# A two-layer trunk on one core: the second expert stage's rows fetched by index from memory, retention's queries and keys in seven half products, and the first attention weights loaded in halves

## The chip, the cores and the metric

The kernel runs on one core of one Trainium2 chip. The metric is the device time of one execution in microseconds (us). The engines are TensorE (PE in the profile, with its weight loads PEld), VectorE (DVE), ScalarE (ACT), GpSimd (POOL) and the SyncE queue (SP), which only issues transfers here. All data is float32.

## What is computed

```python
def trunk(x, cond, ...):                       # 128 context tokens and 256 sample tokens, D = 1024
    for i in range(2):
        sh1, sc1, g1, sh2, sc2, g2 = ada_modulation(cond, w_ada[i], b_ada[i])
        h = rmsnorm(x, norm_mix_g[i]) * (1 + sc1) + sh1
        mix = diff_attention(h, ...) if i == 0 else retention(h, ...)
        x = x + g1 * mix
        h = rmsnorm(x, norm_ffn_g[i]) * (1 + sc2) + sh2
        x = x + g2 * group_moe(h, w_router, router_bias, moe_w_gate[i], moe_w_up[i], moe_w_down[i])
    return rmsnorm(x, final_norm_g), ...

def retention(h, w_qkv, w_g_f, w_g_b, ...):    # 4 heads, query and key width 256, value width 512
    q, k, v = split(h @ w_qkv); g_f = silu(h @ w_g_f); g_b = silu(h @ w_g_b)
    # forward and backward chunk scans of q, k, v, normed, gated, then @ w_o

def group_moe(h, ...):                         # 16 experts; each token goes to its two best
    s = sigmoid(h @ w_router)                  # of one group of four
    for e in range(16):
        y += (silu(h @ wg[e]) * (h @ wu[e]) * gate[:, e]) @ wd[e]   # wg, wu: 1024 x 512, wd: 512 x 1024
```

## The kernel before

The 384 tokens are held as three tiles of 128. `hT` holds the normed activations with the features on the partitions, in 8 pieces of 128 features (`kt`). The stages follow one another: start and modulation, differential attention of 8 heads, output projection, first expert stage (layer 0), retention of 4 heads, output projection, second expert stage (layer 1), final norm.

**Weights.** They stream through `ring`, six slots of 2 MiB, and in the expert stages through three more places (`sq`, `hT` and parts of `work`). `plan_units` writes the order and the slot of every load by hand, and the SP queue issues the loads in that order, each after the wait that frees its slot. In an expert stage the load number 3e, 3e+1, 3e+2 is gate, up and down of expert e. Loads up to number 35 cycle through nine places and the rest through six: gate and up of expert e free their places when its activations have been transposed (`T`), down when its last product is done (`down`). So the loads of expert 14 wait for `T` of expert 12, and the gate and up loads of expert 15 for `T` of expert 13.

**PSUM.** There are 8 banks. `plan_jobs` lists every use of a bank in TensorE's order; `open_job` waits until the bank's tenant of eight jobs before has been evacuated.

**Expert stage** (`experts`). Each expert takes a block of 64 token rows. TensorE gathers the rows of two experts at once, by a product of the token rows `htok` with a 0/1 matrix `sel` that VectorE makes (`gather`, line 986: 8 feature pieces by 3 token tiles); ScalarE copies the result into `xs`. For each expert it then computes gate and up together on the two halves of the array (lines 1089 and 1090, 8 steps), ScalarE takes the silu (line 1463), VectorE multiplies (line 1969), TensorE transposes the result (line 1103), ScalarE copies that (line 1466), and TensorE forms the down product (lines 1120 and 1121), which VectorE copies out (line 1975) and ScalarE stores to memory (line 1475). The gather of the next pair's rows is cut in two: three of four pieces of a half stand between the gate and up products and the transposes, the fourth between the transposes and the down product. TensorE runs its program in order, so these are what fills the two waits. Experts with more than 64 tokens run extra blocks (`overflow`, lines 1014 to 1043): experts 4, 5, 6 and 7 in layer 1, five blocks in all. Experts 14 and 15 are combined on the chip (line 1060, with VectorE's additions at line 1901, as side work between the gate and up steps of expert 15); the others' rows are fetched back at the end by six indexed transfers that POOL issues (line 2168).

**Retention.** Per head h, TensorE first forms queries and keys with the features on the partitions: `to_features` (line 771), four tiles of 128 features by 384 tokens, 8 steps each. Then come the values `rv` and the gates `rg` 0 and 1 by `seven_products`: one tile of tokens by a plain product (`to_tokens`, line 808), the other two tiles by a seven-product scheme for 2 x 2 blocks (line 786: 7 products of 4 steps and 256 columns) on sums of the operands. VectorE forms the sums (`weight_sums`, line 2003; once for the activations at lines 2035 to 2040) and joins the products (`join`, line 2012), for which ScalarE keeps the first product (`m1`, line 1524). Each half product has a bank of its own. After that come the scores, states and outputs of the head (lines 1164 to 1198), with VectorE's statistics (lines 2086 to 2101). The sums live in ring slots 4 and 5, so four slots (`RSLOT`) turn in this stage.

The matmuls are in float32, which the profile shows as two records each; a transpose is one record.

## Time and profile before

| | |
|---|---|
| median of 3 runs | 1441.8 us (1439.5 to 1443.28) |
| the profiled execution | 1440.93 us, its span 1439.0 us |
| PE busy | 1354.5 us, 94% of the span |
| DVE busy | 517.8 us, 36% |
| ACT busy | 282.2 us, 20% |
| POOL busy | 47.2 us, 3% |
| mean TensorE clock | 0.983 of full speed |
| moved by transfers | 344.83 MB, mean 240 GB/s |

The span runs from the first to the last instruction; the time lies 1.93 us above it. A busy PE is a PE with a matmul in flight: consecutive matmuls overlap in the records, so the cost of one is read from the distance of starts and not from its mean duration. A transfer's duration runs from its issue to its landing and holds its time in the queue.

### The profile page before, as it was taken

To read this page: it belongs to the slowest core of one execution; us is meant where nothing else is said; L and a number is where in the kernel's file an instruction comes from. 1 tells how busy PE (TensorE), PEld (TensorE's weight loads), DVE (VectorE), ACT (ScalarE), POOL (GpSimd) and SP (SyncE) were. 2 spreads that over 40 slices of the span, in tenths; PEclk is the share of its full clock that TensorE was granted. 3 is DMA by queue.
4 is the path that set the end of the run, shared out by engine and by line. 5 is a ranking of instruction groups with operands and counts; after the bars stand their busy time and mean duration, and the time that the engine had idled before them with its cause. 6 is when DMAs were issued, how large, how long until landed. Compare 5 with 4: busy or idle time off the path is not lost.

```text
span 1439.0 us, 17852 instructions
## 1 busy us (share of the span) xinstructions
PE 1354.5 (94%) x6816; PEld 768.3 (53%) x6816; DVE 517.8 (36%) x1376; ACT 282.2 (20%) x580; POOL 47.2 (3%) x63
## 2 busy tenths in 40 slices
PE   5899999997998999889999999999998998899997
PEld 2456556555444444447667567576565544444434
DVE  3145355625111111554464653744513311111123
ACT  3143344411010111231120221212111100001013
POOL 1001200000000000100000000100100000000010
PEclk9999999998999999999999999999999899999998
DMA  9967686926999999912323423224534799579891
GB/s 363 322 244 231 224 279 237 380 95 238 392 396 350 398 395 378 388 64 94 117 82 117 146 88 110 95 89 139 182 118 174 254 398 387 190 258 398 324 399 52
DMA packets 162742, 344.83 MB, mean 240 GB/s; under 512 B 5929, under 2 KB 23554, under 8 KB 162626
## 3 DMA queue, kind: packets, MB, share of 16 engines
q1 hardware_dynamic: 150320, 319.19, 60.4%
q10 hardware_dynamic: 9362, 14.37, 2.7%
q0 software_dynamic: 2944, 9.65, 2.5%
q8 instruction: 82, 1.34, 0.4%
q14 instruction: 34, 0.28, 0.1%
HBM read 324.96 MB, written 18.22 MB: 238 GB/s over the span
## 4 chain that ended last, share of the span: by engine, by line
PE 85%; DMA 6%; DVE 4%; ACT 2%; SPq 2%; issue 1%; DVEq 0%; ACTq 0%
PE psum L1089 14%; PE psum L771 11%; PE psum L786 10%; PE psum L808 9%; PE psum L1120 7%; PE psum L986 7%; PE psum L1206 5%; PE psum L937 3%; PE psum L1198 3%; DMA ring<-in_moe_w_up 3%; PE psum L673 2%; PE psum L1031 2%; DMA ring<-in_da_w_qkv 2%; SPq L569 1%; PE psum L1060 1%
## 5 line engine op out<-in xcount | busy, mean ns | idle before, releaser
L771 PE MATMUL psum<-hT,ring 128*128 128x384 f32 x512 | 173.5, 498 | 8.8 <-DMA ring<-in_da_w_qkv 5.9
L1089 PE MATMUL psum<-ring,work 128*64 128x512 f32 x384 | 170.1, 593 | 2.6 <-DMA ring<-in_moe_w_up 2.6
L1090 PE MATMUL psum<-ring,work 128*64 128x512 f32 x384 | 170.2, 594 | 0.0
L771 PEld LDWEIGHTS psum<-hT,ring 128*128 128x128 f32 x512 | 99.0, 195 | 77.4 <-issue 8.3
L808 PE MATMUL psum<-ring,hT 128*128 128x512 f32 x288 | 125.9, 593 | 0.0
L986 PE MATMUL psum<-work 128*128 128x128 f32 x768 | 106.4, 292 | 5.5 <-issue 3.5
L1089 PEld LDWEIGHTS psum<-ring,work 128*64 128x64 f32 x384 | 51.8, 137 | 111.2 <-issue 111.0
L986 PEld LDWEIGHTS psum<-work 128*128 128x128 f32 x768 | 95.0, 200 | 28.2 <-issue 24.0
L1120 PE MATMUL psum<-ring,work 128*64 128x512 f32 x192 | 89.9, 612 | 1.3 <-issue 1.2
L1975 DVE COPY work<-psum 128x512 f32<-128x512 f32 x32 | 22.1, 692 | 191.2 <-PE psum L1121 191.2
L1121 PE MATMUL psum<-ring,work 128*64 128x512 f32 x192 | 90.0, 613 | 0.0
L1969 DVE TENSOR_TENSOR work<-work,psum 64x512 f32<-64x512 f32 x32 | 22.1, 690 | 187.1 <-ACT work L1463 187.0
L808 PEld LDWEIGHTS psum<-ring,hT 128*128 128x128 f32 x288 | 54.8, 190 | 63.7 <-issue 62.1
L786 PE MATMUL psum<-ring 128*128 128x256 f32 x384 | 86.8, 379 | 0.0
L1463 ACT ACTIVATE work<-psum 64x512 f32<-64x512 f32 x32 | 18.8, 588 | 314.8 <-PE psum L1090 314.8
L786 PEld LDWEIGHTS psum<-ring 128*128 128x128 f32 x384 | 73.1, 190 | 9.8
L786 PE MATMUL psum<-ring,hT 128*128 128x256 f32 x288 | 66.1, 379 | 0.0
L2003 DVE TENSOR_TENSOR ring<-ring 128x1024 f32<-128x1024 f32 x48 | 60.8, 1283 | 2.5 <-DVE work L2012 1.3
L786 PEld LDWEIGHTS psum<-ring,hT 128*128 128x128 f32 x288 | 54.8, 190 | 12.5 <-issue 5.7
L1640 DVE SCALAR_TENSOR_TENSOR xT<-psum,mod,xT 128x128 f32<-128x128 f32 x70 | 24.7, 412 | 94.7 <-PE psum L1206 62.1
L1090 PEld LDWEIGHTS psum<-ring,work 128*64 128x64 f32 x384 | 51.9, 137 | 0.0
L1120 PEld LDWEIGHTS psum<-ring,work 128*64 128x64 f32 x192 | 24.9, 140 | 47.2 <-issue 45.0
(338 smaller groups left out, 1810.0 us busy)
## 6 DMA issues: line engine op xcount, KB each, us to landing
ring<-in_w_ada SPq DMA_DIRECT2D x24, 2048.0 KB, 12.4
ring<-in_moe_w_gate SPq DMA_DIRECT2D x24, 2048.0 KB, 13.0
ring<-in_moe_w_up SPq DMA_DIRECT2D x24, 2048.0 KB, 17.4
ring<-in_moe_w_down SPq DMA_DIRECT2D x24, 2048.0 KB, 17.9
ring<-in_da_w_qkv SPq DMA_DIRECT2D x6, 2048.0 KB, 14.8
sq<-in_moe_w_gate SPq DMA_DIRECT2D x8, 1536.0 KB, 12.3
hT<-in_moe_w_up SPq DMA_DIRECT2D x8, 1536.0 KB, 15.0
work<-in_moe_w_down SPq DMA_DIRECT2D x24, 512.0 KB, 11.3
```

Source lines behind the costliest of these rows:

```text
L771: last = mm(b[:, 0:TOK], w[:, kt, col:col + P], hT[:, kt, :], start=kt == 0, stop=kt == KT - 1)
L786: last = mm(b[:, 0:256], rows[k], weights[k], start=k == 0, stop=k == 3)
L808: last = mm(b, hT[:, kt, P * t:P * t + P], w[:, kt, :], start=kt == 0, stop=kt == KT - 1)
L937: last = mm(b[:, 0:TOK], w[:, h, P * (ft % 4):P * (ft % 4) + P], oT[:, h, :], start=h == 0, stop=h == HEADS - 1)
L986: last = mm(out, htok[:, t, P * kt:P * kt + P], sel[:, t].rearrange("p x s -> p (x s)"), start=t == 0, stop=t == TT - 1)
L1089: mm(psum[0:BLK, x, :], xk, wg[kt], start=kt == 0, stop=kt == KT - 1)
L1090: last = mm(psum[BLK:P, x, :], xk, wu[kt], start=kt == 0, stop=kt == KT - 1)
L1120: mm(psum[0:BLK, 5 + x, :], eaT[:, x, k, :], wd[k][:, 0:512], start=k == 0, stop=k == 3)
L1121: last = mm(psum[BLK:P, 5 + x, :], eaT[:, x, k, :], wd[k][:, 512:D], start=k == 0, stop=k == 3)
L1198: last = mm(b, a, v, start=n == 0, stop=n == len(terms) - 1)
L1206: last = mm(b[:, 0:TOK], w[:, k, P * (ft % 2):P * (ft % 2) + P], roT(k), start=k == rows[0], stop=k == rows[-1])
L2003: V.tensor_tensor(wT_[:, part], x, y, ALU.subtract).then_inc(wT_ready, 1)
```

## The change

- **Second expert stage.** `htok` is also written to a new table `token_rows` in memory. For the pairs of experts 1 to 7, TensorE multiplies `sel` by a column of token numbers (`list_tokens`), VectorE copies the 128 row numbers, POOL issues an indexed fetch of 128 rows of 4 KiB (`row_loads`), and TensorE transposes the rows (`turn_rows`, 8 transposes). The gather by products is left for pair 0 and for layer 0. `xs` is no longer double.
- **Fillers.** For odd experts of layer 1, and for expert 15 of layer 0, the first three of eight gate and up steps are put before the end of the expert ahead: two between its gate and up products and its transposes, one between the transposes and the down product. For odd experts of layer 1 the turned rows of the next pair (6 and 2) stand at these places. The side work of expert 15 moves from steps 1, 3, 5, 7 to steps 4, 5, 6, 7.
- **Queries and keys of retention** come by seven products too, with 192 columns each (the token axis is halved at 192), after `rv`; two half products share a bank. New sums of the weights (`feature_sums`) take ring slot 1, so three slots turn, and the order of loads and jobs follows. VectorE's joins of these write `rq` and `rk`, scaled, instead of four ScalarE copies.
- **First weights.** The loads `("q", 0)` and `("k", 0)` are issued as two halves of 256 columns each, in the order q, k, table, q, k; the first two heads' projections wait for the first halves.

```diff
+AHEAD = 3
-    plan = {(e, 2 * i + 1): pair(e - 1, i) for e in range(LAST + 1, NE) for i in range(4)}
+    plan = {(e, AHEAD + 1 + i): pair(e - 1, i) for e in range(LAST + 1, NE) for i in range(4)}
-RSLOT = 4
+RSLOT = 3
-        jobs += [(("rq", h, t), "act") for t in range(2)] + [(("rk", h, t), "act") for t in range(2)]
-        jobs += seven(("rv", h), "dve") + seven(("rg", h, 0), "act") + seven(("rg", h, 1), "act")
+        jobs += seven(("rv", h), "dve") + seven(("rq", h), None) + seven(("rk", h), None)
+        jobs += seven(("rg", h, 0), "act") + seven(("rg", h, 1), "act")
...
                     if name == ("q", 0):
-                        sp.dma_start(att_tab, att_d).then_inc(in_att, 16)
+                        for half in range(2):
+                            for kind in "qk":
+                                here = slice(256 * half, 256 * half + 256)
+                                to, src = source((kind, 0))[0]
+                                sp.dma_start(to[:, :, here], src[:, :, here]).then_inc(slot_full[slot_of[(kind, 0)]] if half else in_first[kind], 16)
+                            if half == 0:
+                                sp.dma_start(att_tab, att_d).then_inc(in_att, 16)
...
+            def seven_features(kind, h):
...
+                product(1, of_w(0, low), of_h(low, early_))
+                product(2, of_w(0, high), of_h(high, early_))
+                if h == 0 and j == 0:
+                    pe.wait_ge(hF_ready, 5)
+                pe.wait_ge(fS_ready, 4 * (2 * h + j) + 4)
+                product(3, of_fS(1), of_hF(1))
...
+                def list_tokens(q):
+                    pe.wait_ge(m["sel"], q + 1)
+                    if q > 1:
+                        pe.wait_ge(m["listed"], q - 1)
+                    chosen = sel_second if q == 1 else sel
+                    for t in range(TT):
+                        last = mm(psum[:, 4, 0:1], chosen[:, t].rearrange("p x s -> p (x s)"),
+                                  table(base_sb, base_at, "token")[:, t:t + 1], start=t == 0, stop=t == TT - 1)
+                    last.then_inc(m["ids"], 1)
+                def turn_rows(q, kts):
+                    pe.wait_ge(m["rows"], 16 * q)
+                    pe.wait_ge(m["xs"], 2 * q)
+                    for kt in kts:
+                        last = tr(psum[:, 2 + kt // 4, P * (kt % 4):P * (kt % 4) + P], xrow[:, P * kt:P * kt + P], ident)
...
+                            pipelined = lambda n: n % 2 == 1 and (l == 1 or n == NE - 1)
+                            gate_up(e, range(AHEAD if pipelined(e) else 0, KT // 2))
+                            hint = pe.mark_branch_hint_location()
+                            wg, wu = gate_up(e, range(KT // 2, KT))
                             overflow(e, wg, wu, hint)
                             more = q + 1 < NE // 2
-                            if more:
+                            if pipelined(e + 1):
+                                gate_up(e + 1, range(AHEAD - 1))
+                            if more and l == 0:
                                 pe.wait_ge(m["sel"], q + 2)
                                 pe.wait_ge(m["xs"], q * 2 + x + 1)
                                 gather(x, range(4 * x, 4 * x + 3))
+                            if more and l and x:
+                                if q + 2 < NE // 2:
+                                    list_tokens(q + 2)
+                                turn_rows(q + 1, range(6))
                             pe.wait_ge(m["gated"], e + 1)
...
+                            if pipelined(e + 1):
+                                gate_up(e + 1, range(AHEAD - 1, AHEAD))
...
             for h in range(RH):
-                unit_wait(pe, ("rqk", h))
-                for t in range(2):
-                    to_features(("rq", h, t), w, P * t, 2 if h == 0 and t == 0 else None)
-                for t in range(2):
-                    to_features(("rk", h, t), w, RDK + P * t)
...
                 seven_products(("rv", h), 3 * h)
+                unit_wait(pe, ("rqk", h))
+                seven_features("rq", h)
+                seven_features("rk", h)
...
+            def feature_sums(kind, h):            # 4 sums of 128 x 512
...
+                V.tensor_tensor(to[:, 0], a21, a22, ALU.add).then_inc(fS_ready, 1)
+                V.tensor_tensor(to[:, 2], a11, a21, ALU.subtract).then_inc(fS_ready, 1)
...
+            def join_features(kind, h, to):       # 7 additions of 128 x 192
...
+            V.tensor_tensor(hF[0], b12, b11, ALU.subtract).then_inc(hF_ready, 1)
...
+            feature_sums("rq", 0)
...
                     if h + 1 < RH:
-                        weight_sums(("rv", h + 1), ((0,), (1,), (2, 3))[t])
+                        if t < 2:
+                            weight_sums(("rv", h + 1), ((0, 1), (2, 3))[t])
+                        else:
+                            feature_sums("rq", h + 1)
...
+            def row_loads():
+                m = M[1]
+                pool.wait_ge(m["kept"], 32)
+                for q in range(1, NE // 2):
+                    pool.wait_ge(m["listed"], q)
+                    if q > 1:
+                        pool.wait_ge(m["gathered"], 2 * q)
+                    pool.indirect_dma_start(out=xrow, out_offset=None, in_=token_rows_d,
+                                            in_offset=bass.IndirectOffsetOnAxis(ap=ids[:, q:q + 1], axis=0)).then_inc(m["rows"], 16)
```

## Rows read from the trace of the kernel before

**Rows 1.** Windows by stage: length, busy of PE, PEld, DVE, ACT, POOL, clock, DMA share, GB/s.

```profile
343.50:599.50 256.00, 243.51 (x1473) 113.68 (x1472) 44.97 (x112) 31.12 (x56) 5.73 (x6) 0.99 0.99 375
618.20:1046.00 427.80, 427.16 (x1504) 278.35 (x1504) 226.35 (x574) 83.05 (x168) 15.84 (x12) 1.00 0.32 110
1126.40:1412.00 285.60, 264.21 (x1811) 122.12 (x1810) 49.48 (x117) 33.98 (x66) 5.76 (x6) 0.99 0.85 320
```

**Rows 2.** PE's timeline at the start: start, length; in brackets the idle time before.

```profile
36.61 7.12 PE L771 MATMUL psum<-hT,ring 128*128 128x384 f32 x16 [2.56 <-DMA ring<-in_da_w_qkv]
47.03 7.12 PE L771 MATMUL psum<-hT,ring 128*128 128x384 f32 x16 [3.30 <-DMA ring<-in_da_w_qkv]
54.42 20.76 PE L808 MATMUL psum<-ring,hT 128*128 128x512 f32 x48
```

**Rows 3.** Two loads of line 569, issued at 25.2 (k) and 28.0 (v).

```profile
DMA to landing us min/median/max: 21.8/23.1/24.4
```

**Rows 4.** Timelines of PE and DVE where retention's first head begins.

```profile
618.26 22.34 PE L771 MATMUL psum<-hT,ring 128*128 128x384 f32 x64 [1.85 <-DVE hT L1625]
623.17 4.88 DVE L2003 TENSOR_TENSOR ring<-ring 128x1024 f32<-128x1024 f32 x4 [0.53 <-DVE hT L1625]
629.89 0.69 DVE L2040 TENSOR_TENSOR ring<-hT,ring 128x512 f32<-128x512 f32 x1
```

**Rows 5.** PE's timeline where retention's second head begins.

```profile
716.87 20.80 PE L771 MATMUL psum<-hT,ring 128*128 128x384 f32 x64
737.51 7.03 PE L808 MATMUL psum<-ring,hT 128*128 128x512 f32 x16
744.37 3.62 PE L786 MATMUL psum<-ring,hT 128*128 128x256 f32 x16
747.83 5.34 PE L786 MATMUL psum<-ring 128*128 128x256 f32 x24
```

**Rows 6.** DVE's timeline there: second and third part of the next weight sums.

```profile
721.96 1.23 DVE L2003 TENSOR_TENSOR ring<-ring 128x1024 f32<-128x1024 f32 x1
731.45 3.44 DVE L2003 TENSOR_TENSOR ring<-ring 128x1024 f32<-128x1024 f32 x2
```

**Rows 7.** PE's timeline in the second expert stage, expert 2.

```profile
1161.25 2.27 PE L986 MATMUL psum<-work 128*128 128x128 f32 x18
1163.45 0.46 PE L1103 MATMUL psum<-base_sb,work 64*128 64x64 f32 x4
1163.84 0.94 PE L986 MATMUL psum<-work 128*128 128x128 f32 x6
```

**Rows 8.** PE's groups by line, retention's 48 transposes: busy, mean ns, idle before.

```profile
L1153 PE MATMUL psum<-base_sb,work 128*128 128x128 f32 x48 | 6.3, 274 | 0.6 <-DVE work L2110 0.6
```

**Rows 9.** PE's timeline, transposes of expert 14 in layer 0, with no filler.

```profile
574.12 0.43 PE L1103 MATMUL psum<-base_sb,work 64*128 64x64 f32 x4 [1.50 <-DVE work L1969]
```

**Rows 10.** Windows of experts 5 and 10 of layer 1.

```profile
1206.60:1242.30 35.70, 29.55 (x326) 14.93 (x324) 6.47 (x17) 2.32 (x5) 0.00 (x0) 1.00 0.56 204
...
1318.60:1332.50 13.90, 13.90 (x78) 6.51 (x76) 2.11 (x4) 1.57 (x3) 0.00 (x0) 1.00 1.04 396
```

**Rows 11.** SP's timeline: first load after `T` of expert 7, and of expert 12.

```profile
1286.66 0.37 SPq L603 DMA_DIRECT2D ring<-in_moe_w_gate  x1
...
1360.55 0.37 SPq L603 DMA_DIRECT2D ring<-in_moe_w_gate  x1
```

**Rows 12.** The chain of waits at the end of either expert stage.

```profile
561.86 18.42 DMA ring<-in_moe_w_up
...
590.50 0.90 PE psum L1060 x4
...
1374.94 17.66 DMA ring<-in_moe_w_up
...
1402.81 0.90 PE psum L1060 x4
```

**Rows 13.** The six indexed transfers of line 2168 at the end of layer 1, from 1387.4 on.

```profile
DMA to landing us min/median/max: 8.3/10.9/11.7
```

237 lines of the change are left out of this document (170 added, 67 removed).

## The prediction

> **What bounds the kernel now.** I read the windows by stage first. Retention holds TensorE for 427.16 of 427.80 us while the transfers move 110 GB/s, so there a microsecond of matmul is a microsecond of time. The first expert stage moves 375 GB/s with the transfer engines 99% busy, the second 320 GB/s with TensorE busy for 264.21 of 285.60 us [rows 1]. The windows of single experts say which of the two limits the second stage: expert 10 takes 13.9 us at 396 GB/s, expert 5, with its two extra blocks, 35.7 us at 204 GB/s [rows 10]. An expert's three loads and its stored block are 6.29 + 0.26 = 6.55 MB, which at 396 GB/s take 16.5 us, 5.5 us a load. So even now an ordinary expert uses weights faster than they come (13.9 against 16.5), and only the slack gathered during experts 4 to 7 keeps TensorE fed. The chain of waits confirms it: at the end of both stages stands the landing of expert 15's up weights, at 1392.60 in layer 1 and at 580.28 in layer 0 [rows 12]. A shorter TensorE program pays until the stream of weights binds, and no further. I sum the parts against the profiled execution (1440.93 us, 0.9 below the median of 1441.8).
>
> **First weights.** TensorE waits 2.56 us for q and 3.30 us for k [rows 2]. With half of each (1 MB, 2.7 us at the 375 GB/s of rows 1) ahead of the rest, q is there when `hT` is, and k follows at once, so k is done by about 49. But v was issued at 28.0 and landed 24.4 later, at 52.4 [rows 3], behind the same bytes as before, and its products began at 54.42 [rows 2]. They can begin 2.0 us earlier and no more. The two projections took 7.12 us each for 16 records against 5.2 at full rate [rows 5]: after each wait the clock was halved, which costs up to 1.9 us. The new wait ahead of v, some 3 us, can cost that again. Term: 0 to -2, I take -1.
>
> **First expert stage, expert 15.** The gathers stay. New is that two gate and up steps of expert 15 stand ahead of the transposes and the down product of expert 14. Its up weights land at 580.28, paced by loads and not by TensorE, and today expert 14 is finished in the wait. Now everything of it is queued behind that landing. From the landing: 2 steps 1.7, transposes of 14 and of its weights 0.9, one step 0.9, down 3.4, steps 3 and 4 1.7, then four pieces of side work; each needs VectorE's two additions of the piece before, so one follows another at best every 1.8 us, and the last ends 6.3 later: 14.9. Before, the last piece ended at 591.4 [rows 12], 11.1 after the landing. That is +3.8, and the 7.8 us for which TensorE now stands still (572.6 [rows 9] to 580.4) should be followed by half clock, +1.7 (rows 2 showed 1.9). The price of this part is bounded by 0 (if the steps were already there) and +8 (if the additions come every 2.7). I take +5.5.
>
> **Retention.** A head's queries and keys are now 64 records of 384 columns, 20.64 us or 0.3225 each; 512 columns take 0.429, 256 take 0.216 [rows 5], 128 take 0.122 [rows 7]. The new 2 x 28 matmuls are 112 records of 192 columns. No row has that width; the slope from 256 gives 0.162, the line between 128 and 256 gives 0.169: 18.2 to 18.9 us, a gain of 1.7 to 2.5 a head, 6.8 to 9.9 over four. I take 8.3. VectorE's new work per head, 8 sums of 128 x 512 at about 0.61 (4 of 1024 take 4.88 [rows 4]) and 14 additions of about 0.35, makes 10 us; it had 226 of 428 us busy [rows 1] and stays below 65%. What could surface is lateness. From the second head on, `rv` follows the outputs directly: its third product falls at 716.87 + 6.9 + 3.5 = 727.2. Its weight sums are now made in the first two visits, done at 721.96 + 2.5 = 724.4 [rows 6], before that. The feature sums take the third visit, 731.45 + 2.5 = 734, and are wanted at 716.87 + 19.5 + 2.7 = 739. Hidden by 3 to 5 us; if a visit slips by more, TensorE waits. At the first head it is not hidden: `rv` comes to product 3 at 618.26 + 6.9 + 3.5 = 628.7, the sums are ready at 630.6 [rows 4], a wait of 1.9 where the waits for `hT` had cost 1.6 (22.34 - 20.80), and perhaps half clock. With that +0.3 to +2. One slot less costs nothing: a head uses five loads in some 105 us at 8 us each. Banks are not short, since a unit now takes 4 or 5 instead of 8. Term: -7, bounds -10 and -3.
>
> **Second expert stage, up to expert 7.** Per expert the gather is 18 records before the transposes (2.20 us) and 6 after (0.87) [rows 7]. Up to the transposes of expert 7 go 8 x 2.20 + 7 x 0.87 = 23.7. Added are five lists of 6 records and 4 x 6 + 3 x 2 transposes, at 0.13 a record [rows 8]: 3.9 + 3.9. The fillers must still cover 1.50 us ahead of the transposes [rows 9]: two steps, 1.7, do for even experts, list and six transposes, 1.57, for odd ones. Behind the transposes two records stand where six stood (0.26 us for 0.87); how much of the 0.87 is needed no row shows, so it costs 0 to 0.6 each time; I take 0.3, three times. Net -15.0. The store of `htok` and the first fetch lie beside pair 0 (15 us and more before the rows are wanted). So `T` of expert 7 comes at 1271.7 instead of 1286.7 [rows 11], TensorE-bound.
>
> **From there the loads bind.** Up to expert 15's up weights there are 17 loads, 17 x 5.5 = 93.5. The start of the stream costs 4.5 (before, 5 loads from 1360.55 to 1392.60 took 32.0, 27.5 by rate). Three fetches of rows of 0.52 MB: 4.0. That gives 1373.7. POOL's six final fetches (3.15 MB, 7.9 us at 396) start about 8 us after expert 13's down product, as before (1387.4 [rows 13]), but now that is ahead of this landing and not behind it; sharing costs it 0 to 7.9, I take 4: 1378. With the 14.9 from above and 1.7 for half clock the last side work ends at 1394.3 instead of 1403.7: -9.4. Bounds: no sharing, no half clock and 5.4 a load give -17; full sharing and 5.7 a load (396 GB/s less the waits between releases) give -2.
>
> By the Trainium skill, DMA: Bandwidth & Descriptors, section Queues, rings and completion order, each DMA engine goes round robin between the queues that have work; that would put the sharing near its full 7.9 and layer 1 at -5.5. Before, the load behind the landing, with the six fetches beside it, cannot be told apart in these rows.
>
> **Sum.** -1 + 5.5 - 7 - 9.4 = -11.9; 1440.9 - 11.9 = 1429.0, and 1429.9 on the scale of the median. I say 1429.5.
>
> **Rivals.** (A) TensorE's saving counts in full in the second stage: seven pairs at 4.3, 30 us, so about 1408. For it speaks that TensorE is busy for 264 of 286 us; against it the 16.5 us a set of weights needs. It wants 6.55 MB in 11.7 us, 560 GB/s, and no row has more than 396. 3%. (B) The stream eats it: full sharing (the round robin above), 5.7 a load, and retention at its short bound: -1 + 7 - 3 - 3 = 0, 1437.5 to 1442. 15%. (C) Slower: the fetched rows come late. A pair has some 23 us between the last transposes of one fetch and the first of the next, a fetch landed in 8.3 to 11.7 us beside weights [rows 13]. From 23 us on, each further microsecond costs seven; at 26 us the gain is gone twice over, near 1450. 5%. By the Trainium skill, SBUF — State Buffer, section SBUF: two separate sides, POOL can't write descriptors while VectorE holds the shared port in its fast two-port modes; in these rows VectorE is busy for 49 of 286 us, so the slack covers it. (D) VectorE binds in retention: a join slips behind the sums and TensorE waits 3 us a head; retention gives nothing, 1437. 12%. (E) The sum above, 65%: its own range 1420 to 1437.
>
> **Range and chances.** (E) with the better part of (B) and (D) gives 1418 to 1440. A difference of 0.3%, 4.3 us, is about what can be told from no change. (A), most of (E), half of (D) and a third of (B) are faster by more: 0.76; what is left of (B), (D) and the edge of (E) lies within, 0.17; (C) and the tail of (B) are slower, 0.07.
>
> **What would show it.** q and k back to back, v at 52.4; in layer 0 TensorE idle from 572 to 580 ahead of expert 15, whose end is 4 to 6 us later after the landing; records of 192 columns at 0.16 to 0.17; a wait of about 2 us for the sums in head 0 and none later; experts 0 to 7 of layer 1 shorter by 15 us, then waits for up weights at experts 13 and 15 of 8 us and more with 390 GB/s throughout. Wrong it becomes if the weight stream is faster or slower than 5.5 us a load, if the last fetches don't share, or if VectorE is late at the turn of heads.

## The result and the profile after

The changed kernel takes 1454.0 us (median of 7 runs, 1445.8 to 1458.2) beside 1441.8 for the kernel before on the same chip: the ratio is 1.0067 (95% interval 1.0046 to 1.0088). It is slower by 0.67%, where 1429.5 and "faster" had been predicted. Windows of the changed kernel's profiled execution (span 1453.4 us, against 1439.0), the same three stages as in [rows 1]:

```profile
343.50:621.50 278.00, 251.76 (x1476) 119.39 (x1475) 45.51 (x115) 31.10 (x56) 5.75 (x6) 0.95 0.95 357
640.76:1120.00 479.24, 477.69 (x1923) 336.06 (x1924) 273.30 (x693) 83.72 (x169) 16.03 (x12) 1.00 0.34 116
1140.00:1426.40 286.40, 238.95 (x1566) 97.68 (x1565) 51.98 (x135) 32.57 (x66) 12.27 (x13) 0.95 0.90 336
```

In the second expert stage TensorE has 238.95 us of work instead of 264.21, yet the stage is no shorter, and in both expert stages the granted clock is 0.95 instead of 0.99. The saving of matmul work was made, and spent on waiting. To see where, I cut both traces at the same events (starts of the first expert's silu, of the transposes `T` of experts 4, 7 and 13, of the copy `y` of expert 15, of retention's first product, of the first transpose of `htok`):

| us | before | changed | difference |
|---|---|---|---|
| start to first expert | 355.1 | 356.4 | +1.3 |
| to `T` of expert 4 | 57.7 | 64.9 | +7.2 |
| to `T` of expert 13 | 148.0 | 146.7 | -1.3 |
| to `y` of expert 15 | 38.9 | 53.5 | +14.6 |
| to retention | 18.5 | 19.2 | +0.7 |
| retention, to `htok` of layer 1 | 489.1 | 479.8 | -9.3 |
| to first expert of layer 1 | 26.2 | 26.4 | +0.2 |
| to `T` of expert 7 | 152.6 | 138.3 | -14.3 |
| to `T` of expert 13 | 87.8 | 86.2 | -1.6 |
| to `y` of expert 15 | 38.2 | 54.9 | +16.7 |
| to the end | 26.9 | 26.9 | 0 |

Three lines carry the loss: both ends of an expert stage, and a place early in layer 0 where nothing had been changed. Start of the changed kernel, TensorE's timeline, against [rows 2]:

```profile
36.11 12.25 PE L801 MATMUL psum<-hT,ring 128*128 128x384 f32 x32 [1.49 <-DVE hT L1728]
53.25 22.53 PE L873 MATMUL psum<-ring,hT 128*128 128x512 f32 x48 [4.46 <-DMA ring<-in_da_w_qkv]
```

q and k run back to back, as predicted, but v starts only 1.2 us earlier, after a wait of 4.46 (its load went out behind the halves, at 34.7 us instead of 28.0, and landed at 53.2), and its 48 records take 22.53 instead of 20.76. The gain is used up by 76 us.

Retention's second head, TensorE's timeline, against [rows 5]:

```profile
753.05 1.89 PE L817 MATMUL psum<-ring,hT 128*128 128x256 f32 x8
754.78 1.89 PE L817 MATMUL psum<-ring 128*128 128x256 f32 x8
756.50 2.76 PE L848 MATMUL psum<-hT,ring 128*128 128x192 f32 x16
759.11 1.46 PE L848 MATMUL psum<-ada_rows,ring 128*128 128x192 f32 x8
...
764.30 4.06 PE L848 MATMUL psum<-hT,ring 128*128 128x192 f32 x24
```

A record of 192 columns takes 0.163 us (16 in 2.61, from start to start), and no wait stands between the products. The two scaled units run from 756.50 to 774.71, 18.2 us instead of 20.6.

The place in layer 0 where nothing was changed, TensorE's timeline ahead of expert 3's gathers; first the kernel before:

```profile
396.69 2.28 PE L986 MATMUL psum<-work 128*128 128x128 f32 x18
```

and the same 18 records in the changed kernel:

```profile
402.68 4.18 PE L1053 MATMUL psum<-work 128*128 128x128 f32 x18 [3.53 <-issue]
```

TensorE stands for 3.53 us and waits for nothing that the profile shows, and the gathers behind it take 4.18 instead of 2.28, at half clock (1.2 GHz instead of 2.4: the granted clock is 0.50 from 401.4 to 408.2 us). The kernel before has a stall of this kind too, at another place, between `T` of expert 7 and `T` of expert 13 of layer 1:

```profile
1343.20 1.38 PE L986 MATMUL psum<-work 128*128 128x128 f32 x10 [2.50 <-issue]
```

The end of layer 0, the chain of waits in the changed kernel, against [rows 12]:

```profile
569.03 21.40 DMA ring<-in_moe_w_up
590.57 1.08 PE psum L1174
591.69 0.81 PE psum L1174
...
594.25 0.62 PE psum L1205 x4
...
601.99 0.84 PE psum L1127 x4
...
603.85 1.38 PE psum L1127 x4
...
608.09 0.85 PE psum L1127 x2
...
611.09 3.38 issue
614.48 0.66 PE psum L1205 x4
```

The matmuls of the first early step are 0.86 us apart instead of 0.43: half clock. Expert 14's transposes start at 594.25, 20.1 us later than in [rows 9], then its down product, then the side work (line 1127), and at the end a second stall of issue. TensorE's timeline there shows the idle time ahead of the early step and ahead of expert 15's transposes:

```profile
590.57 1.08 PE L1174 MATMUL psum<-ring,work 128*64 128x512 f32 x1 [10.79 <-DMA ring<-in_moe_w_up]
...
614.48 0.66 PE L1205 MATMUL psum<-base_sb,work 64*128 64x64 f32 x4 [5.01 <-issue]
```

The end of layer 1, the chain of waits:

```profile
1372.51 26.69 DMA ring<-in_moe_w_up
1399.34 1.09 PE psum L1174
...
1403.02 0.62 PE psum L1205 x4
...
1410.85 0.84 PE psum L1127 x4
...
1416.95 0.85 PE psum L1127 x2
```

The same, with a load that takes 26.69 us where it took 17.66. The two ends divide like this (us from the start of `T` of expert 13; the second stretch ends with the last record of side work):

| | layer 0 before | layer 0 changed | layer 1 before | layer 1 changed |
|---|---|---|---|---|
| to the landing of 15's up weights | 19.4 | 22.4 | 18.7 | 27.7 |
| to the end of side work | 11.1 | 19.0 | 11.1 | 19.1 |
| to `y` of expert 15 | 8.4 | 12.1 | 8.4 | 8.1 |

The first of the six indexed fetches of results went out 9.0 us (layer 0) and 14.0 us (layer 1) ahead of that landing, where it had been 6.0 and 5.2.

### The profile page after: what moved, and what is told of

It is laid out like the page before. It is cut to its first block, busy times and chain, and to the rows that moved or that the text cites. A ratio compares the mean times of both kernels' runs of the same rounds, so it can differ in the third digit from the quotient of the medians.

```text
span 1453.4 us, 17927 instructions
## 1 busy us (share of the span) xinstructions
PE 1330.3 (92%) x6770; PEld 775.9 (53%) x6770; DVE 557.7 (38%) x1476; ACT 276.2 (19%) x572; POOL 54.0 (4%) x70
## 3 DMA queue, kind: packets, MB, share of 16 engines
q8 instruction: 82, 1.34, 0.4%
## 4 chain that ended last, share of the span: by engine, by line
PE 78%; DMA 8%; DVE 5%; SPq 5%; ACT 2%; issue 2%; DVEq 0%; ACTq 0%
PE psum L1174 13%; PE psum L817 10%; PE psum L873 8%; PE psum L1226 6%; DMA ring<-in_moe_w_up 5%; PE psum L848 5%; PE psum L801 5%; PE psum L1308 5%; PE psum L1053 4%; PE psum L1004 3%; PE psum L1300 3%; SPq L633 2%; PE psum L703 2%; PE psum L1098 2%; DMA ring<-in_da_w_qkv 1%
## 5 line engine op out<-in xcount | busy, mean ns | idle before, releaser
L1174 PE MATMUL psum<-ring,work 128*64 128x512 f32 x384 | 178.1, 610 | 38.3 <-DMA ring<-in_moe_w_up 36.8
L1175 PE MATMUL psum<-ring,work 128*64 128x512 f32 x384 | 178.2, 610 | 0.0
L873 PE MATMUL psum<-ring,hT 128*128 128x512 f32 x288 | 129.2, 605 | 6.3 <-DMA ring<-in_da_w_qkv 4.5
L1226 PE MATMUL psum<-ring,work 128*64 128x512 f32 x192 | 90.7, 617 | 2.7 <-issue 2.5
L1227 PE MATMUL psum<-ring,work 128*64 128x512 f32 x192 | 90.9, 618 | 0.0
L801 PE MATMUL psum<-hT,ring 128*128 128x384 f32 x256 | 86.7, 494 | 2.6 <-DVE hT L1728 1.5
L1570 ACT ACTIVATE work<-psum 64x512 f32<-64x512 f32 x32 | 18.9, 589 | 298.2 <-PE psum L1175 298.2
L1053 PE MATMUL psum<-work 128*128 128x128 f32 x432 | 62.8, 303 | 6.6 <-issue 4.6
L801 PEld LDWEIGHTS psum<-hT,ring 128*128 128x128 f32 x256 | 48.8, 193 | 34.4 <-issue 3.2
L1053 PEld LDWEIGHTS psum<-work 128*128 128x128 f32 x432 | 57.0, 212 | 18.4 <-issue 15.2
L1226 PEld LDWEIGHTS psum<-ring,work 128*64 128x64 f32 x192 | 25.6, 141 | 52.4 <-issue 51.3
## 6 DMA issues: line engine op xcount, KB each, us to landing
ring<-in_w_ada SPq DMA_DIRECT2D x24, 2048.0 KB, 12.8
ring<-in_moe_w_up SPq DMA_DIRECT2D x24, 2048.0 KB, 17.8
ring<-in_moe_w_down SPq DMA_DIRECT2D x24, 2048.0 KB, 18.9
work<-in_moe_w_down SPq DMA_DIRECT2D x24, 512.0 KB, 12.1
```

The source lines that it names most:

```text
L801: last = mm(b[:, 0:TOK], w[:, kt, col:col + P], hT[:, kt, :], start=kt == 0, stop=kt == KT - 1)
L873: last = mm(b, hT[:, kt, P * t:P * t + P], w[:, kt, :], start=kt == 0, stop=kt == KT - 1)
L1053: last = mm(out, htok[:, t, P * kt:P * kt + P], sel[:, t].rearrange("p x s -> p (x s)"), start=t == 0, stop=t == TT - 1)
L1174: mm(psum[0:BLK, x, :], xk, wg[kt], start=kt == 0, stop=kt == KT - 1)
L1175: last = mm(psum[BLK:P, x, :], xk, wu[kt], start=kt == 0, stop=kt == KT - 1)
L1226: mm(psum[0:BLK, 5 + x, :], eaT[:, x, k, :], wd[k][:, 0:512], start=k == 0, stop=k == 3)
```

## The experiments

The kernels ran in five sets, each set on a chip of its own with the kernel before beside it (medians 1442.0 to 1443.9); the ratio is to that, with its 95% interval. Between kernels of different sets, the difference of the medians and that of the ratios part by some 2 us. My theory was that expert 15's early steps put expert 14 behind a landing; the rivals were the stream itself (more traffic, shared engines), retention, and TensorE's stalls of issue.

**Expert 15 in the old order**, changed kernel otherwise:

```diff
-    plan = {(e, AHEAD + 1 + i): pair(e - 1, i) ...
+    plan = {(e, 2 * i + 1): pair(e - 1, i) ...
...
-                            pipelined = lambda n: n % 2 == 1 and (l == 1 or n == NE - 1)
+                            pipelined = lambda n: n % 2 == 1 and l == 1 and n < NE - 1
```

> The changed kernel with expert 15's steps and side work back in their old order, in both layers; experts 1 to 13 of layer 1 keep their fillers. Theory (fillers ahead of a landing): expert 14 is again finished while TensorE would wait for expert 15's up weights, so y of expert 15 comes 19.5 to 21 us after that landing, as before, and no longer 31.1 and 27.2: -11 in layer 0, -7 in layer 1, about 1435, a few us faster than before. Rival 1 (the loads themselves got slower through the fetched rows): the landings, 21.4 and 26.7 us after their issue, set the end whatever the order; at most -5, 1449. Rival 2 (retention and instruction supply): no change in either stage's end, 1453.

1444.3 us, ratio 1.0005 (0.9987 to 1.0023): ten less than the changed kernel, as fast as before but not faster. `T` of 13 to `y` of 15: 43.6 in layer 0 (-9.9), 51.7 in layer 1 (-3.2). The direction is the theory's, the size is not, and the rival of the late landing holds in part: the up weights of layer 1 landed 27.3 us after issue here too, with the fetches 14.7 us ahead. Part of the shortfall lies where the edit changed nothing: the first half of layer 1 (to `T` of expert 7) took 145.4 us instead of 138.3, with a stall of issue of 4.09 us at 1151.9.

**Fetches later**, changed kernel otherwise; POOL also waits for expert 15's up weights:

```diff
                 pool.wait_ge(m["o_stored"], total * 64 + 64)
+                unit_wait(pool, ("moe", l, 3 * (NE - 1) + 1))
```

> The changed kernel, but the six indexed fetches of results at the end of each layer start only when expert 15's up weights have landed. Theory: the fetches took 2 us (layer 0) and 5.6 us (layer 1) of the weights' stream ahead of that landing; the up weights land 5.5 to 6 us after the gate weights in both layers, the order of expert 14 behind them stays, and the kernel gains 6 to 8: about 1447. Rival (what delays the landing is the issue of the load, not what shares the engines): the distance of gate and up stays at 7.9 and 11.2, and the time at 1454.

1443.7 us, ratio 1.0001 (0.9987 to 1.0015): -10.3, more than expected. TensorE's program is that of the changed kernel. Up weights of layer 1 landed 21.35 us after issue instead of 26.69, those of layer 0 18.76 instead of 21.40. The ends are 48.4 us long in layer 0 (-5.1) and 49.0 in layer 1 (-5.9).

**The early steps of expert 15 alone, in the kernel before:**

```diff
-    plan = {(e, 2 * i + 1): pair(e - 1, i) ...
+    plan = {(e, AHEAD + 1 + i): pair(e - 1, i) ...
...
+                            pipelined = lambda n: n == NE - 1
+                            gate_up(e, range(AHEAD if pipelined(e) else 0, KT // 2))
+                            hint = pe.mark_branch_hint_location()
+                            wg, wu = gate_up(e, range(KT // 2, KT))
...
+                            if pipelined(e + 1):
+                                gate_up(e + 1, range(AHEAD - 1))
...
+                            if pipelined(e + 1):
+                                gate_up(e + 1, range(AHEAD - 1, AHEAD))
```

> The kernel before, with nothing of the change but expert 15's three early steps and its side work at steps 4 to 7, in both layers. Theory: this part alone costs what the two stage ends lost. Up weights land at 580.3 and 1392.6 as before, the last side work ends 17.6 us later instead of 11.1, and y of expert 15 27 to 31 us later instead of 19.5: +8 to +12 in each layer, 1458 to 1465. As predicted at first: +5.5 and about as much again, 1453. Rival (the loss needs the row fetches of layer 1 or the new retention): within 3 us of the kernel before.

1468.4 us, ratio 1.0179 (1.0161 to 1.0197): 24.5 slower, above even that. The ends are 50.3 (+11.4) and 47.3 (+9.1) long, but expert 3 of layer 0 had the stall of 3.3 us too, though no step there was moved (+6.2 up to `T` of expert 4): only the waits for its weights are issued twice, since `gate_up` is called in two parts.

**Retention and the first weights alone** (changed kernel with both expert stages as before: gathers by products, no fetched rows, `pipelined` never):

> The changed kernel with both expert stages as before (gathers by products, no fetched rows, no early steps): left are the retention part and the first weights in halves. Theory: -7 to -9 from retention, 0 from the first weights: 1433 to 1435. Rival (retention lost by VectorE's new work or by idle time at the turn of heads): 1439 or more.

1445.0 us, ratio 1.0008 (0.9989 to 1.0027). The expected 1434 didn't come. But the trace clears retention: 479.8 us, -9.3, as in every kernel with it. The gain was lost elsewhere: +2.7 to the first expert, +6.0 up to `T` of expert 4 with the same stall of 3.31 us, +10.5 at the end of layer 0 with no early step at all. Of these 10.5, 3.3 lie ahead of the landing of the up weights (fetches 9.3 us ahead) and the rest behind it, with 5.78 us of stall ahead of expert 15's transposes where the kernel before waits 2.29. Something that had been no part of any theory was common to all kernels but the one before.

**No work changed.** The kernel before with the eight steps issued from two calls, so that two fulfilled waits are repeated at an expert's middle:

```diff
-                            wg, wu = unit(e, 0), unit(e, 1)
-                            for kt in range(KT):
...
+                            pipelined = lambda n: False
+                            gate_up(e, range(AHEAD if pipelined(e) else 0, KT // 2))
+                            hint = pe.mark_branch_hint_location()
+                            wg, wu = gate_up(e, range(KT // 2, KT))
```

> The kernel before, with the eight gate and up steps of an expert issued from two calls, so that the two waits for its weights (long fulfilled) are issued a second time at its middle; no work is added, left out or moved. Theory (place of the code): TensorE's idle time of 3.3 to 3.6 us ahead of expert 3's gathers in layer 0, put down to issue, and half clock behind it came with every kernel so built and not with the one before, so here too expert 3's transposes come 4 to 5 us late; 0 to +6 in all, 1443 to 1449. Rival (the early steps themselves cause it): the first expert stage as before up to expert 13, within 1 us.

1452.1 us, ratio 1.0076 (1.0055 to 1.0097): above the range expected and as slow as the changed kernel, with the stall of 3.69 us at expert 3 and one of 5.69 ahead of expert 15's transposes. The rival falls.

**Early steps for experts 1 to 11 of layer 1 alone, fetches later or not:**

```diff
+                            pipelined = lambda n: n % 2 == 1 and l == 1 and n < NE - 4
```

> The changed kernel with early steps for experts 1 to 11 of layer 1 alone (13 and 15 in the old order, in both layers), and with the last six fetches started when expert 15's up weights have landed. Theory: T of expert 12 no longer waits for expert 13's up weights, so the loads of 14 go out some 10 us earlier; no expert is queued behind a landing; from T of expert 13 to y of expert 15 41 to 44 us in both layers. Against the run that only delayed the fetches -6 in layer 0 and -8 to -11 in layer 1: 1425 to 1431. Rival (layer 1 is held by the bytes alone, whatever the order): only the ends gain, 1436 or more.

> As the run with early steps for experts 1 to 11 of layer 1 alone, but with the last six fetches started as in the changed kernel. Theory: -10 to -14 in layer 0's end and in layer 1 together beside the kernel with early steps up to 13 costing nothing more: 1430 to 1437; the difference to its sister with late fetches is the price of sharing, 2 us in layer 0 and 4 to 6 in layer 1. Rival (T of expert 12 waits for nothing that matters): as the run without expert 15's early steps, 1444.

1429.5 us, ratio 0.9921 (0.9899 to 0.9942), with the later fetches; 1443.3, ratio 1.0000 (0.9984 to 1.0016), without. Both have the same program on every engine but POOL. The first is in its range. The second is above its own, 1430 to 1437, since sharing cost more than the 2 and 4 to 6 us expected. Expert 15's up weights in the chain of waits, first with the later fetches, then without:

```profile
1358.26 23.02 DMA ring<-in_moe_w_up
```

```profile
1368.33 29.68 DMA ring<-in_moe_w_up
```

In layer 0 it is 17.8 and 22.2. So of the 13.7 us some 11 are the shared stream. The stalls of issue come at the same four places in both, within 1.6 us of each other, and the first half of layer 1 differs by 3.0 us (142.8 and 145.8).

**TensorE kept busy in the wait.** Steps whose result is used nowhere, on expert 14's weights into the bank that expert 15 overwrites, in the changed kernel:

```diff
+                            if e == NE - 2:
+                                for n in range(34 if l else 24):         # second run: 16 if l else 12
+                                    xk = xs[:, 0 if l else q % 2, n % KT, 0:BLK]
+                                    mm(psum[0:BLK, 1, :], xk, wg[n % KT], start=True, stop=True)
+                                    mm(psum[BLK:P, 1, :], xk, wu[n % KT], start=True, stop=True)
```

> The changed kernel, with 48 (layer 0) and 68 (layer 1) matmuls added ahead of expert 15's early steps, on expert 14's weights into the bank that expert 15 overwrites; their result is used nowhere. They take 10.3 and 14.6 us and so lie in TensorE's idle time of 10.8 and 15.2. Theory: with no idle time the clock isn't halved, and the steps, transposes and the down product behind the landing run at full rate: 2 to 3 us less per layer, 1448 to 1451. Rival (half clock there costs nothing, since VectorE's additions set the pace): no change, 1454.

> As the run with added matmuls ahead of expert 15's early steps, but with 12 steps (layer 0) and 16 steps (layer 1) instead of 24 and 34: a step takes 0.86 us, so the first attempt held TensorE for 20.6 and 29.2 us, past the landing. Now 10.3 and 13.7, inside the idle time of 10.8 and 15.2. Theory: what the first attempt showed behind its last added step (24.5 us to y of expert 15 instead of 31.0 in layer 0, clock 1.00) comes now without the overshoot; half clock behind the wait is worth 3 to 4 us a layer: 1446 to 1450. Rival: the order alone sets the time, 1454.

The first run, 1469.9 us (1.0194, 1.0171 to 1.0218), missed: I had taken a step for 0.43 us, it is two pairs of records of 0.43, and the steps ran 11 us past the landing. But the granted clock behind them was 1.00 (window of 600 to 612 us), and expert 15's `y` came 24.5 us after the last added step instead of 31.0 after the landing. The second, 1447.5 (1.0035, 1.0016 to 1.0055), is 6.5 below the changed kernel, as expected. In it `y` of expert 15 came 24.6 us (layer 0) and 24.5 us (layer 1) after the landing of the up weights, where the changed kernel takes 31.1 and 27.2. But in layer 0 the added instructions also took away the stall ahead of expert 15's transposes (1.76 us of waiting for VectorE, where there had been 5.01 of issue). So only the 2.7 us of layer 1, where that wait is 1.76 us in both, can be put to the clock.

**Waits issued once** (the second and later parts of an expert's steps skip them), in the best kernel so far and in the changed kernel, and then **the first weights whole** as before:

```diff
+                def unit(e, part, wait=True):
...
+                    if wait:
+                        unit_wait(pe, name)
...
+                    wg, wu = unit(e, 0, kts[0] == 0), unit(e, 1, kts[0] == 0)
```

> As the best run so far (early steps for experts 1 to 11 of layer 1 alone, late fetches), but an expert's two waits for its weights are issued once, by its first step, and not with every part: up to 30 instructions less per layer on TensorE's queue, no other difference. Theory (place of the code): the idle time put down to issue moves or shrinks; in layer 0 expert 3's 3.4 us and the 5.4 us ahead of expert 15's transposes go back to none and 2.3, and the time is 5 to 9 lower, 1421 to 1425. Rival (those stalls come from the loads beside them, not from the code): unchanged, 1429.5.

> The changed kernel with nothing different but that an expert's waits for its weights are issued once, by its first step. Theory (place of the code): up to 9 us of the changed kernel's loss are stalls of issue at expert 3 (3.5) and ahead of expert 15's transposes (5.0) in layer 0, with half clock behind; 1445 to 1450. Rival: unchanged, 1454.

> As the run with waits issued once, and the first weights of q and k loaded whole as before. Theory: the halves cost 1.3 us (start to first expert: 355.4 to 357.8 us in seven runs with them, 354.7 to 355.1 in three without) and gave nothing; 1 to 2 less than its sister, which 5 rounds can hardly tell; in the trace v's products follow k's without the 4.5 to 7 us of idle time. Predicted at first: the halves gain 1, so this is 1 slower.

1432.7 (0.9928, 0.9903 to 0.9952) and 1456.9 (1.0095, 1.0072 to 1.0117): no gain in either, and both expectations missed; the 3 us by which the medians are higher are within what two sets differ by. With the first weights whole the first of them takes 1420.4 (0.9851, 0.9827 to 0.9874), 12.3 less than its sister of the same set and not the 1 to 2 expected: the stall at expert 3 is gone, and the wait ahead of expert 15's transposes is 2.29 us long in both sisters, as in the kernel before (that much of the expectation was met). The halves add two semaphore instructions to TensorE's program before the experts. Are those 12 us the loads or the two instructions?

**Fulfilled waits added** at the start of TensorE's program, where it waits for data anyway: four to the kernel before, two and 32 to the best kernel.

```diff
             pe.wait_ge(in_x, 32)
+            for _ in range(4):               # 2 and 32 in the other two
+                pe.wait_ge(in_x, 32)
```

> The kernel before with four more waits on TensorE's queue at its start, each for a semaphore that is already there; nothing else. Theory (place of the code): TensorE has 162 semaphore instructions before the branch of expert 3 in layer 0 where the 3.4 us stall doesn't come, and 164 to 168 where it does, so four more waits bring it: start to T of expert 4 +5 to +6, the whole time +6 to +10, 1449 to 1453. Rival (the stall came with the loads of the halves and with the second waits at expert 3 themselves): 1443, no stall at 400.

> The best kernel (waits once, whole first weights) with two more waits, already fulfilled, at the start of TensorE's queue. Theory (place of the code): it becomes as slow as its sister with the halves, which has the same number of TensorE instructions ahead of the experts: stall at expert 3, 1429 to 1434. Rival (the halves' loads cost the 12 us): 1420 to 1421, as without the waits.

> The best kernel with 32 more fulfilled waits at TensorE's start. They lie in the wait for the first weights and cost nothing themselves. Theory (place of the code): the stalls put down to issue come at other experts than in the best kernel; how long they are isn't known, 1418 to 1435. Rival: the same stalls at the same places and 1420.

1449.9 (1.0046, 1.0027 to 1.0066), 1429.2 (0.9898, 0.9879 to 0.9916) and 1426.0 (0.9876, 0.9856 to 0.9896). Four waits that wait for nothing cost the kernel before, in the same set, 6.6 us. For the best kernel, which ran in another set, two cost 8.8 us by the medians and 0.0047 by the ratios (6.8 us); 32 cost 5.6 us and 0.0025, and there the intervals of the ratios overlap. The trace shows two such waits in one instruction, so the programs are longer by 2, 1 and 16 instructions. TensorE's timeline of the kernel before with four waits more:

```profile
399.41 2.90 PE L988 MATMUL psum<-work 128*128 128x128 f32 x12 [3.56 <-issue]
```

My rule was that 164 to 168 semaphore instructions on TensorE ahead of expert 3 bring the stall there and 162 don't. The trace counts 164 in this run. In the second it counts only 163, and in the third 16 more than in the best kernel; neither has a stall at expert 3. So the expectation of the second run was met in time and missed in place: its stalls are 1.7 to 2.1 us long, one 3.1, and at other experts, and its largest loss, 6.3 us, lies in the first half of layer 1. The best kernel is not free of them either: it has four longer than 1.5 us, all in layer 1, 1.9 to 3.3 us long. TensorE's timeline there:

```profile
1146.34 0.28 PE L1199 MATMUL psum<-base_sb,work 64*128 64x64 f32 x2 [2.09 <-issue]
```

**The change on code that lies well.** The changed kernel with waits issued once and first weights whole (all its early steps, its fetches as they were):

> The changed kernel with waits issued once and first weights whole, so that TensorE's code lies up to expert 3 as in the kernel before; early steps and fetches as in the changed kernel. Theory: no stall at expert 3, first expert 354.7, then the intrinsic price of expert 15's early steps, expert 13's and the shared fetches: 48 to 50 us from T of expert 13 to y of expert 15 in layer 0, 53 to 55 in layer 1; 1440 to 1445, so some 20 above the best kernel and 10 to 14 below the changed one. Rival (the loss is nearly all place of the code): 1425 to 1430.

1437.5 us, ratio 0.9960 (0.9947 to 0.9973), 16.5 below the changed kernel (15.4 by the ratios). Its code lies well only in the sense that the stall at expert 3 is gone; it has three others longer than 1.5 us, of 3.50 us ahead of expert 15's transposes in layer 0 and of 1.96 and 3.38 in layer 1. The last stands between `T` of expert 12 and `T` of expert 13:

```profile
1361.53 0.84 PE L1147 MATMUL psum<-base_sb,work 128*128 128x128 f32 x6 [3.38 <-issue]
```

In the two profiles the difference is 17.8 us. The place at expert 3 gives 7.2 of it, the end of layer 0 5.2, the end of layer 1 8.5 and the start 1.1; the rest is 4.2 longer. And 11.2 of the 13.7 us of the two ends lie ahead of the landing of expert 15's up weights, which the fetches now precede by 5.5 and 6.2 us instead of 9.0 and 14.0.

Then either of two parts undone on it: expert 15 in the old order, and the fetches later.

> The changed kernel with waits issued once and first weights whole, and expert 15 in the old order in both layers; fetches as changed. Theory: the early steps cost 8 to 9 in layer 0 (48.3 us from T of expert 13 to y of expert 15 become 39 to 41) and about 5 in layer 1; 1437.5 - 13 = 1424 to 1427. Rival (on code that lies as before, the order of expert 15 costs no more than the 5.5 predicted): 1431 or more.

> The changed kernel with waits issued once, first weights whole, and the last fetches begun when expert 15's up weights have landed; the early steps as changed. Theory: in the sister without this the fetches started 14 and 6 us ahead of the landing or with it, and the up weights landed 5.7 and 6.3 us after the gate weights, so here little is left to gain: 0 to 3 us, 1434 to 1437. Rival (the fetches always cost their 8 us of the stream): 1430 or less.

1424.7 (0.9870, 0.9850 to 0.9889) and 1437.3 (0.9961, 0.9946 to 0.9975); both as expected. So starting the fetches later gained 10.3 us in the changed kernel and nothing here. TensorE's timelines at the end of layer 0, with the early steps of expert 15:

```profile
580.00 1.09 PE L1166 MATMUL psum<-ring,work 128*64 128x512 f32 x1 [7.28 <-DMA ring<-in_moe_w_up]
...
583.61 0.63 PE L1197 MATMUL psum<-base_sb,work 64*128 64x64 f32 x4
...
590.81 0.92 PE L1119 MATMUL psum<-work 64*128 64x384 f32 x4
...
592.66 1.45 PE L1119 MATMUL psum<-work 64*128 64x384 f32 x4
...
595.05 0.92 PE L1119 MATMUL psum<-work 64*128 64x384 f32 x4
...
596.90 1.45 PE L1119 MATMUL psum<-work 64*128 64x384 f32 x4
601.85 0.66 PE L1197 MATMUL psum<-base_sb,work 64*128 64x64 f32 x4 [3.50 <-issue]
```

and without them:

```profile
575.72 0.43 PE L1197 MATMUL psum<-base_sb,work 64*128 64x64 f32 x4 [1.50 <-DVE work L2077]
...
582.26 0.61 PE L1166 MATMUL psum<-ring,work 128*64 128x512 f32 x1 [1.95 <-DMA ring<-in_moe_w_up]
...
592.27 0.92 PE L1119 MATMUL psum<-work 64*128 64x384 f32 x4
595.48 0.55 PE L1197 MATMUL psum<-base_sb,work 64*128 64x64 f32 x4 [2.29 <-DVE work L2077]
```

The up weights landed 18.9 us after the start of `T` of expert 13 with them and 19.7 without. The last piece of side work starts 16.9 us after the wait's end with them and 10.0 without. The ends of the stages are 48.3 and 46.4 us with them, 39.2 and 38.9 without: 9.1 and 7.5 us. Other stretches are 3.9 us longer without them, at the start and in the first half of layer 1 above all (1.4 each), and the medians differ by 12.8.

## Why the prediction was wrong

**The step that failed** is "First expert stage, expert 15 ... I take +5.5" (bounds 0 to +8), and the same 14.9 us plus 1.7 in layer 1. What was queued behind the landing was named rightly, and TensorE's idle time came as said (7.28 us on well-placed code, 7.8 predicted). The price was too low: 9.1 in layer 0 (from the landing to `y` of expert 15 it took 29.4 us on well-placed code against 19.5), and in the changed kernel that end was 14.6 longer. From the landing to the end of side work it took 18.5 on well-placed code and 19.0 and 19.1 in the changed kernel, against 16.6. The pieces of side work came 1.85 us apart twice, as predicted, and 2.39 once; the early steps ran at half clock for 3.6 us; and behind the gap ahead of expert 15's transposes (3.50 us of issue, where the kernel before waits 2.29) the clock was 0.50 for 6.8 us of the down product instead of 3.4, which had no term. The clock alone was worth more than the 1.7 taken for it: 2.7 in layer 1, by the run with added matmuls.

**What no term held** is the place of TensorE's code. The sum took every instruction for its duration, and a wait that is fulfilled for nothing. The changed kernel is 16.5 us above the same work with waits once and first weights whole, but that difference is not all place of code, since the fetches also fall nearer the landing there. The runs take it apart: with the fetches late the changed kernel takes 1443.7, with waits once and first weights whole on top 1437.3, and without the early steps of experts 13 and 15 on top of that 1420.4. So some 10 us went with the fetches, 6 with the place of the code or the halves, and 17 with those early steps. Why the fetches come nearer the landing in the sister is shown in part: in layer 1 its stall of 3.38 us lies between `T` of expert 12 and `T` of expert 13, which took 13.35 us instead of 10.70, so the loads of 15 went out later. In layer 0 it stays open. What the halves' own loads cost is not told apart from their two waits, since that sister has 164 of the semaphore instructions and the run with added waits 163. That this is the supply of code is argued from the trace, not shown by itself: the profile's page counts 82 transfers and 1.34 MB, so 16 KB each, in the instruction queue of both kernels, and its packets stand where the stalls are; which engine a packet is for, the profile does not tell. In the kernel before one came at 392.6 us, 4 us ahead of expert 3's gathers at 396.7; in the changed kernel it came at 400.0, inside the stall that ends at 402.68; with four waits added at 396.7, the stall ending at 399.41; ahead of expert 15's transposes at 611.8 (614.48). From packet to restart it is 2.7 us each time, and 2.3 to 2.8 at the stalls of the other timelines shown here; the stall of the kernel before at 1343.2 has its packet at 1340.7. Without that stall this stretch, from `T` of expert 7 to `T` of expert 13, takes 83.5 us in the four other kernels that have the old steps there, against 87.8. So the kernel before was itself no neutral measure. Why one or two instructions more make a load late, and which place is good, stays open.

**First weights**, -1 predicted: v began at 53.25 and not at 52.4, and +1.3 remained at the first expert. Wrong in sign and small; but the best kernel was 12.3 us faster without the halves.

**Retention**, -7 predicted: -9.3 up to `htok`, +0.7 ahead of it. Right (479.4 to 481.0 us in every kernel that has it, 489.0 to 490.2 in the others); the first head's wait for the sums was 0.35 us, not 1.9. Rival (D) is out.

**Second expert stage up to expert 7**, -15.0 predicted: -14.3, and -12.8 on well-placed code. Right, but with luck: two kernels with the same work there and other stalls of issue gained only 7.2 (expert 15 in the old order) and 5.7 (waits once). Rival (C), fetched rows too late, is out: they landed in 7.0 to 9.0 us in the changed kernel and no transposes waited for them. Rival (A), the saving in full, is out too: TensorE's work in the stage fell by 25 us and the stage grew by 0.8.

**From there the loads bind**: right in kind, wrong by a size. Relative to the layer's first expert the up weights of 15 landed 6.9 us earlier, not 14.6. TensorE made the sequence 12, 13 in 10.7 us where it had taken 13.9, so the loads of 15 were issued into a fuller queue (gate landed 16.0 after its issue, before 12.54), and the six fetches, begun 14 us ahead of the landing, took their share: gate to up 11.2 us instead of 5.6. I had taken 4 of a possible 7.9 for this. The Trainium skill, DMA: Bandwidth & Descriptors, section Queues, rings and completion order, with its round robin between queues, points to the high end. The trace agrees in direction: between kernels that differ on POOL alone the up weights of layer 1 took 5.3 us longer with the fetches 14.0 us ahead (26.69 against 21.35) and 6.7 with them 16.8 ahead. Where the fetches began only 5.5 us ahead of the landing (well-placed code, layer 0: gate 574.20, up 579.86), gate to up was 5.66 us, with late fetches 5.37, and starting them later gained nothing. So rival (B) was no case by itself, but its mechanism raised the price here.

Added up against the prediction, in us of profile, the changed kernel has: first weights +2.3; layer 0 up to expert 13, which had no term, +5.9; the end of layer 0 +9.1; retention and what surrounds it -1.4; layer 1 +0.8 instead of -9.4, +10.2. That is 26 us, beside the 24.5 between 1429.5 and 1454.0. On well-placed code it is: first weights whole instead of -1, +1.2; expert 15 in layer 0 +3.9; retention and what surrounds it -1.1; layer 1 -4.8 instead of -9.4, +4.6. That is 8.6, beside the 8.0 between 1429.5 and 1437.5, which would have been within the range of 1418 to 1440.

## What to carry to other kernels

Work that is moved ahead to fill a short wait must not itself wait for something later than what it is put before: at the last expert, three early steps for a gap of 1.5 us made the time from that landing to the end of the expert 7 to 10 us longer. Where a stream of loads ends a stage, other transfers belong behind its last critical landing: one wait on POOL was worth 10 and 14 us, where they overlapped with it. And where branches stand in an engine's program, compare a kernel with a twin that has a few idle instructions more before a difference under 1% is explained: here that alone made 6.6 us in the kernel before and some 7 to 9 in the best one. The best kernel (early steps for experts 1 to 11 of layer 1, late fetches, waits once, first weights whole) takes 1420.4 us, 1.5% less than the kernel before.

## What the hardware showed that was not expected

- Two fulfilled waits, one instruction, at the start of TensorE's program cost 8.8 us of 1420 by the medians (6.8 by the ratios), and four, two instructions, cost 6.6 of 1443. 32 of them, 16 instructions, cost 5.6 (3.6 by the ratios, not clear of noise): the cost does not grow with their number.
- A stall put down to issue costs more than its length, through the clock: 3.53 us of idle time, then the granted clock is 0.50 for 6.8 us. The 18 gathers behind it alone ran in 4.18 instead of 2.28 us, and the stretch up to `T` of expert 4 was 7.2 us longer.
- What six indexed fetches (3.15 MB) take from a stream of weights depends on when they begin. From the landing of the gate weights to that of the up weights it was 5.3 to 5.9 us with the fetches behind the landing, 5.6 to 6.3 with them 5.2 to 6.2 us ahead, 7.9 with 9.0, 11.2 with 14.0 and 12.1 with 15.6 us ahead.
